# A mixture-of-experts stage on one core: the expert rows' loads move from SP's queue to ScalarE's

## What is computed

```
lg = x @ w_rg + b_rg;  grp = argmax(lg)                 # one of 4 groups
le_sel = (x @ w_re + b_re)[group grp];  top 2 of its 4 experts
for e in range(16):
    a, u = split(x @ w_gu[e], 2)                        # w_gu[e]: 1024 x 512
    y = y + comb[:, e:e+1] * ((silu(a) * u) @ w_dn[e])  # w_dn[e]: 256 x 1024
```

## Time and profile before

| what | value |
|---|---|
| median of three runs | 712.12 us (709.15 to 714.17) |
| the profiled execution | 710.51 us, its span 708.6 us |
| granted TensorE clock, mean | 0.982 |
| TensorE busy | 663.3 us, 94% of the span |
| VectorE, ScalarE, GpSimd busy | 368.8, 160.2, 95.0 us |
| expert stage | 502.6 us (first gate-up matmul) to 678 us (last down matmul) of the span |
| moved by DMA | 181.46 MB, mean 256 GB/s |

### The profile page before, as it was taken

The page is one execution under the profiler, slowest core; times in us unless marked ns, Lnnn a source line. Parts: engine busy times, 40 slices in busy tenths (PEclk is TensorE's granted clock), DMA queues, the critical chain, the costliest instruction groups (busy, mean ns, idle before and its releaser), DMA issues.

```text
span 708.6 us, 7606 instructions
## 1 busy us (share of the span) xinstructions
PE 663.3 (94%) x2646; PEld 362.3 (51%) x2646; DVE 368.8 (52%) x748; ACT 160.2 (23%) x416; POOL 95.0 (13%) x120
## 2 busy tenths in 40 slices
PE   3799999999999999999999899996999999999993
PEld 3344474345556555577778654443744444444441
DVE  3315562431465655366645636857563445545477
ACT  6000210001222221136655703222200100000113
POOL 1042100112203201020322310121100000000040
PEclk9899999999999999999999999999999999999997
DMA  7988833913015569999952249414899999999573
GB/s 281 387 261 307 322 136 118 358 31 134 31 30 164 229 274 375 421 352 420 420 239 64 87 159 406 176 70 191 303 341 370 389 344 349 346 370 336 208 296 148
DMA packets 63621, 181.46 MB, mean 256 GB/s; under 512 B 5622, under 2 KB 19310, under 8 KB 59492
## 3 DMA queue, kind: packets, MB, share of 16 engines
q1 hardware_dynamic: 54088, 157.53, 61.1%
q0 software_dynamic: 4384, 12.48, 4.9%
q10 hardware_dynamic: 5116, 11.02, 4.0%
HBM read 122.71 MB, written 58.25 MB: 255 GB/s over the span
## 4 chain that ended last, share of the span: by engine, by line
PE 74%; DVE 8%; DMA 8%; SPq 5%; issue 3%; ACT 1%; ACTq 0%; POOL 0%; DVEq 0%; POOLq 0%
PE PS L1645 24%; PE PS L2050 10%; PE PS L1878 7%; PE PS L1637 5%; PE PS L1793 5%; SPq L529 4%; PE PS L2070 4%; DMA RING<-scratch_xs 3%; PE PS L1865 2%; PE PS L1676 2%; DMA PR<-in_w_ada 2%; DMA PR<-scratch_mod 1%; PE PS L1772 1%; PE PS L1586 1%; PE PS L1822 1%
## 5 line engine op out<-in xcount | busy, mean ns | idle before, releaser
L1645 PE MATMUL PS<-RING,hT 128*128 128x512 f32 x400 | 180.7, 600 | 0.8 <-DVE hT L1053 0.8
L1645 PEld LDWEIGHTS PS<-RING,hT 128*128 128x128 f32 x400 | 73.6, 191 | 86.6 <-issue 85.6
L2050 PE MATMUL PS<-PR,RING 128*128 128x512 f32 x192 | 85.3, 593 | 0.6 <-DVE RING L1424 0.6
L1878 PE MATMUL PS<-RING,hT 128*128 128x512 f32 x160 | 72.7, 600 | 0.0
L2050 PEld LDWEIGHTS PS<-PR,RING 128*128 128x128 f32 x192 | 35.7, 190 | 41.4 <-issue 40.7
L1878 PEld LDWEIGHTS PS<-RING,hT 128*128 128x128 f32 x160 | 29.0, 190 | 30.5 <-issue 30.5
L2070 PE MATMUL PS<-PR,TMP 128*128 128x512 f32 x96 | 43.2, 592 | 0.0
L1793 PE MATMUL PS<-RING,hT 128*128 128x256 f32 x160 | 36.9, 384 | 0.7 <-ACT TMP L860 0.6
L1637 PE MATMUL PS<-hT,RING 128*128 128x512 f32 (+3 forms) x128 | 37.1, 450 | 0.0
L949 ACT ACTIVATE TMP<-PS 128x256 f32<-128x256 f32 x16 | 6.1, 384 | 131.5 <-PE PS L2050 131.5
L1030 DVE TENSOR_TENSOR TMP<-PS,TMP 2x512 f32<-2x512 f32 x24 | 16.4, 682 | 36.8 <-PE PS L1676 32.1
(11 more groups left out here) (345 smaller groups left out, 950.0 us busy)
## 6 DMA issues: line engine op xcount, KB each, us to landing
scratch_xs<-fnorm SPq DMA_DIRECT2D x16, 2560.0 KB, 23.6
PR<-in_w_gate_up SPq DMA_DIRECT2D x12, 2048.0 KB, 19.9
PR<-in_w_ada SPq DMA_DIRECT2D x20, 1024.0 KB, 10.4
RING<-in_w_in SPq DMA_DIRECT2D x14, 1024.0 KB, 7.5
PR<-in_w_down SPq DMA_DIRECT2D x12, 1024.0 KB, 23.3
hT<-in_w_gate_up SPq DMA_DIRECT2D x4, 2048.0 KB, 21.8
RING<-scratch_xs SPq DMA_DIRECT2D x56, 128.0 KB, 15.1
scratch_xs<-RING ACTq DMA_DIRECT2D x14, 512.0 KB, 12.5
```

Source lines behind the costliest of these rows:

```text
L1645: last = mm(PS[:, bank, :], hTv[:, k, t * P:(t + 1) * P], ring[:, ci % 2, k, :], start=(k == 0), stop=(k == KD - 1))
L1878: last = mm(PS[:, i % 4, :], hTv[:, k, t * P:(t + 1) * P], ring[:, (WOUT + q) % 2, k, :], start=(k == 0), stop=(k == KD - 1))
L2050: last = mm(PS[:, 4 + b, :], xgT[:, b, k, :], gub[s][:, k, :], start=(k == 0), stop=(k == KD - 1))
```

## The change

SP no longer loads rows in the loop. ScalarE does: after the two silus of a pair and ahead of that pair's two stores it issues eight DMAs (four for each expert) for the experts that take the pair's two slots next. SP's loop has weights alone. Ahead of its loop ScalarE now waits until POOL's scatter has landed, a wait that SP made until now (and still makes for the first loads, which stay with SP).

```diff
@@ SP
             for s0 in (0, 2):
                 for s in (s0, s0 + 1):
                     sp.wait_ge(gu_done[s], qd + 1)
-                    load_x(s, quad * (4 * T - 32) + qd * 32 + s * T)
                     sp.dma_start(gub[s], w_gu[:, bass.ds(quad * 4 + s, 1)].rearrange("p e k n -> p (e k) n")
                                  ).then_inc(wg_in[s], 16)
@@ ScalarE
+        def load_x(s, row):
+
+            for q in range(4):
+                src = scratch["xs"][bass.ds(row, P), 256 * q:256 * q + 256]
+                act.dma_start(xq[32 * q:32 * q + 32, s], src.rearrange("(c j) f -> j c f", j=32)).then_inc(xq_in[s], 16)
+
+        for i, n_ in enumerate((64, 64, 32)):
+            act.wait_ge(h2_sent[i], n_)
         with act.Fori(0, end) as qd:
+            quad = (qd + 1) % QUADS
             for s2 in range(2):
                 silu(qd, s2, 0)
                 silu(qd, s2, 1)
+                for s in (2 * s2, 2 * s2 + 1):
+                    load_x(s, quad * (4 * T - 32) + (qd + 1) * 32 + s * T)
                 store(qd, s2)
```

## The result

The changed kernel takes 727.88 us (median of four runs, 722.98 to 728.73), the kernel before on the same chip 710.63 us: a ratio of 1.025, 95% interval 1.021 to 1.030. The forecast was 714.5 us and its range ended at 724. Lines that differ between the two kernels have moved: 949 is now L948 (silu), 956 L955 (store), 1467 L1477, 1474 L1484, 1477 L1487, 1486 L1496 (`next_rows`), 1495 L1505 (`gated_out`), 1501 L1511, 2050 L2060, 2058 L2068, and ScalarE's row loads are L968.

A forecast was written before the change was run, and what follows sets the result against it. TensorE, busy 94% of the span, was taken to bound the kernel, with DMA saturated from 514 to 664. Sum: 5.1 + 1.0 - 1.4 - 2.3 = +2.4 on 710.5, 712.9, carried to the median as 714.5 us; range 708 to 724.

The forecast's parts named there:

- the first stall: Expert stage, second pair: VectorE waits 9.5 us for rows, its product is 7.5 us late, TensorE stalls 5.1 us.
- the two gains: TensorE's waits of 1.01 and 0.4 us go (1.4 us), and VectorE's 2.3 us wait in the tail goes.
- The price of row packets: Rows between weights on the DMA engines: 1.6 us for 32 row packets, range up to 2.3 us.
- q10 cannot keep up: Rival, chance 0.25: a pair's transfers exceed 21.1 us, VectorE waits at next_rows pair after pair; 724 us.
- in turns they rarely meet each other: Argument against dear rows in ScalarE's queue: row packets taking turns with weights seldom coincide on the engines.
- The turns of one to one: DMA queues alternate by packet whatever its size, so each row packet lets one weight packet by.
- the first landing: Second pair: the second expert's rows are through at 554.4 and landed at 555.4 us.
- That the weights never leave a gap: First stall: the second expert's 32 row packets also meet 32 weight packets, 15.0 + 1.6 us.
- Once: Later pairs take 20.7 us against 21.1, so TensorE's 5.1 us stall does not recur; 1 us for bad turns.
- 1 us for the stores behind the rows: VectorE's gated_out waits about 1 us for the first pair's stores, which stand behind rows in q10.
- ScalarE's queue: Eight issues cost 3.8 us, covered; rival, chance 0.1: the queue fills or issues cost more, silus run late, 722 us.
- The rows get through quickly: Rival, chance 0.15: several row packets pass per turn, rows land in time, only the gains stay; 708.4 us.

The follow-up runs named there:

- e14: Changed kernel with only ScalarE's row loads written to all 128 partitions, SP's first loads still to 32; 707.58 us, ratio 0.998.
- e1: Changed kernel with ScalarE's rows as whole rows of 4 KB, 32 rows in each DMA, a quarter of the packets; 726.26 us, ratio 1.026.
- e5: Changed kernel with each row DMA, ScalarE's and SP's first ones, written to all 128 partitions in 1 KB packets; 710.18 us, ratio 1.006.
- e15: Changed kernel with each row DMA writing 32 partitions that lie 4 apart, SP's first loads too; 715.11 us, ratio 1.009.
- e8: Changed kernel, but the rows loaded during the first pair stay with SP; 730.12 us, ratio 1.029.
- e2: Changed kernel with all rows issued by GpSimd in a queue of their own, the first experts' too; 719.67 us, ratio 1.020.
- e7: Kernel before, rows from SP, with each row DMA written to all 128 partitions in 1 KB packets; 707.51 us, ratio 0.999.
- e3: Changed kernel with only the first expert's rows of each pair on ScalarE, the second's left with SP; 707.04 us, ratio 0.999.
- e6: Changed kernel with one row DMA per expert, 128 packets of 4 KB to 128 partitions, for both engines' loads; 707.05 us, ratio 1.000.
- e10: Changed kernel with each row DMA writing 64 neighbouring partitions, SP's first loads too; 729.0 us, ratio 1.029.
- e12: Changed kernel with one DMA per block of 32 rows, a quarter of each row to each of 128 partitions, SP's first loads too; 790.61 us, ratio 1.118.

## Why the prediction was wrong

In the terms of the prediction's sum: the first stall was 5.7 us (forecast 5.1), everything behind it 8.9 us more of idle (forecast 1.0), the lower clock 6.4 us (no term), and the two gains, 1.4 and 2.3 us, came.

**The price of row packets** is the step that failed ("I take 1.6 us for 32, nearer to the lower end, because the slow rate belongs to stretches in which all engines write the same 32 partitions at once"). Their own time was right: 188 packets of q10 in 6.1% of 9 us of 16 engines are 47 ns each, 1.5 us for 32. But the weights taken in turn with them slow down. From 523 to 532 us q1's 3.24 MB in 92.0% of 9 us are 2.56 us per MB, against 2.35 for gate-up alone and 2.38 in e14. From 532 to 541 q1 has 3.01 MB at 93.0%, 2.78 us per MB. More of that is down weights, in packets of 8 KB, and such a mix costs 2.44 in e14 (1.11 MB at 90.3% from 532 to 535). On the 6.3 MB of 32 weight packets that is 1.3 to 2.1 us, so 32 row packets cost 2.8 to 3.6 us in all, not 1.6, and 64 cost 5.6 to 7.2. The rival "q10 cannot keep up" decides from 3.6 us. The reason given against it, "in turns they rarely meet each other", is what e1, e5 and e14 refute: the rows needn't meet each other, they hold up the weights.

**The turns of one to one** held, 68 to 68, and so did the first landing roughly: 559.0 instead of 555.4, two experts at some 1.8 us each more, which lies within the 1.3 to 2.1 us above.

**That the weights never leave a gap** was the other half of the first stall ("the second expert's 32 row packets also meet 32 weight packets"), and it failed by the forecast's own prices. e14 has those prices: turns of one to one and weights at nearly their full speed. There q1 runs empty for part of 535 to 538, the second expert's rows pass in that gap, and VectorE waits for no rows at all. So with row packets as cheap as assumed the stall of 5.1 us need not come. In the changed kernel the slowed weights fill the gap, and the stall comes. That its size was nearly met is in part luck: two errors went against each other. e15, with full-speed weights too, does show the forecast's picture (VectorE waits 11.94 us, 9.5 forecast; TensorE 5.6 us in all, 5.1 forecast; 715.1 us, 714.5 forecast), but with dearer issues and a later start. The turns alone are thus worth between nothing (e14) and 7 us (e15), by margins of a few us in time, and the slow narrow writes make up the rest of the 17.

**"Once"** failed. There are three stalls, 14.6 us. The third has the same links as the first two, three pairs of experts further on: rows late by 5.7 us at 630.1, then waits for stores of 1.6 and 3.1 us. e8 shows that it isn't the queue at the start of the stage.

**"1 us for the stores behind the rows"** failed: 11.0 us of waits in `gated_out` in five places. The two in the second pair come from stores that took up to 37.81 us to land. The rival had this mechanism, with about 3 us.

**ScalarE's queue.** The eight issues at 3.8 us were right for the first pair (3.83). "Q10 holds at most one pair of rows and two of stores" counted what a pair brings, not what was still there when it landed late: the later issues took 19.55 and 12.03 us and, in e8, 22.43. So the sign of this rival came, but its mechanism didn't decide: the hold ended at 561.17, before VectorE's result was there, and e2 loses 2% without row loads on ScalarE.

**The clock** was missing from the sum: 6.4 us, more than the first stall itself (6.2 of them in the three groups behind the stalls). A stall of 5 us costs more than 5 us here, as the rows at 0.50 show. The sum had a term for idle time and none for what comes behind it.

**Right:** SP's earlier weights were worth nothing beyond the 1.4 us; the added wait for the scatter cost nothing (ScalarE waited until 510.0 and its first silu began at 513.32, before 513.51); the 2.3 us of the tail came. Of the signs that the prediction named for being right, VectorE's wait near 546 came (13.1 us instead of 9) and TensorE idle by 561, and so did the sign for the slower case, DMA issues of several us on ScalarE. The rival "The rows get through quickly" fell: ScalarE's row loads took up to 34.7 us from issue to landing.

Why the kernel before doesn't suffer, though it writes the same narrow rows: there they stood in SP's queue, first in, first out, and what they held up was weights, which had 20 us in which to land early. e7 makes that reserve larger (gate-up lands in 11.9 us) and gains nothing. The change gave the reserve to the weights (11.3 us), which don't need it, and took it from rows and stores, which are needed within one pair. e3, at 356 GB/s and without loss, fits this: a pair's second rows still go ahead of weights. That this is the whole of it is an argument from e3, e7 and e14, not a measurement of its own. No version tried beats the kernel before by more than its interval.

## What to carry to other kernels

Before a small transfer is moved out of the queue of a large one, ask which of the two has slack: queues take turns by packet, so 1 KB packets get one turn each against 16 KB, and everything queued behind them waits too. Look at which partitions a DMA writes: 32 or 64 neighbours slow the other queue's packets as well. Full-width writes made the same move free (e6, e14; 0.6% in e5), and every fourth partition brought the loss from 2.5% to 0.9%. And price a TensorE stall with the clock behind it, from a row at the low level.

## What the runs showed of the hardware that was not expected

- Rows of 1 KB that write 32 neighbouring partitions cost about as much in another queue's packets as in their own: 1.3 to 2.1 us beside 1.5 us for 32 in turn with 32 weight packets. A saturated window had 376 GB/s, 410 to 413 with all 128 partitions (e5, e14), 412 with 32 spread out (e15), 383 with 64 neighbours (e10).
- Turns go by single packets, whatever their number in a DMA: in e1, where a row DMA has 2 data packets of 4 KB for each engine and a gate-up DMA 8, 59 packets of q10 passed with 63 of q1 from 526 to 529 us.
- The issuing engine is held when much is still under way in its queue: 19.55 us for eight issues with about ten DMAs of 8 packets for each engine outstanding; 20.01 us for four with 32 packets each (e12). This looks like a limit near 100 packets for an engine, an estimate from these two cases (about 11 x 8 and 3 x 32) that no run tested further; e1's eight issues, with 2 packets each, took 3.83 to 4.15 us throughout.
- A DMA of the same bytes on every fourth partition or on 64 cost SP 0.66 us to issue, not 0.46 (5.27 or 5.28, and 3.66 us for eight).
- A DMA whose source has an outermost dimension of 4 kept a quarter of the engines busy, 90 GB/s.
- After idle of 4 to 6 us TensorE's eight matmuls took 6.39 and 5.93 us instead of 3.60, at a granted clock of 0.50.
